# The first block's opening reordered by halves of the features

## The chip, the cores and the metric

The kernel runs on one core of one Trainium2 chip. The metric is device microseconds for one execution; lower is better. Engines are named as in the profile: PE is TensorE (PEld its weight loads), DVE is VectorE, ACT is ScalarE, POOL is GpSimd, SP is the engine that issues most transfers.

## The reference, cut to what matters

The kernel computes three transformer-like layers over 512 tokens of 1024 features. Only the opening of the first one matters here:

```python
mod = jax.nn.silu(c) @ w_ada + b_ada              # 1024 -> 3*1024
shift, scale, gate = jnp.split(mod, 3, axis=-1)
h = rms_norm(x, norm_g) * (1 + scale[:, None, :]) + shift[:, None, :]
proj = h @ w_in                                    # q, keys, values, gates, u, z
...
# u (512 columns) feeds the S5 mixer: tables from a_re, a_im, log_dt, b, c
lam_bar = jnp.exp(lam * dt)
b_bar = ((lam_bar - 1.0) / lam)[..., None] * lax.complex(b_re, b_im)
```

Products with `w_in` are made exact enough in float32 by splitting both operands into a rounded part (`hi`, type fp32r) and a remainder (`lo`), and adding three products: hi·hi, lo·hi, hi·lo.

## The kernel before

Each engine has its own list of instructions, written out by hand and run in order; semaphores join the lists. `x` comes in four token tiles of 128 rows. Features are counted in `KD` = 8 groups of 128, `k` = 0 to 7, so "the first half" is `k` = 0 to 3 (features 0 to 511).

**Modulation.** `w_ada` is cut into six pieces of 512 columns, 2048 KB each. Pieces 0 and 1 are the shift for the first and second half of the features, 2 and 3 the scale. `times_c` multiplies one piece by silu(c) on PE; ACT copies the resulting row out (`move_rows`, L676) and PE turns it into columns of `bank[4]` (`mod_columns`, with `ones`). DVE's `modulate` adds biases and writes `hT = hT * modA + modS`, one group `k` at a time (L1853, semaphore `h_raw`).

**Normalised x.** ACT squares the four token tiles with a running sum (L667, `ss`); POOL makes the inverse root (L539, L540); DVE scales (`normal`, L1803, `xn_ready`); PE transposes (L1133, `xT_done`); ACT moves the result to `hT` (L683, `xT_evac`).

**Splitting.** For each weight piece `n`, ACT writes `p_hi(n)` (L723) and DVE `p_lo(n)` (L1772). ACT rounds `hT` into `x_hi` (L731, `h_hi`), DVE writes the remainder into `hT_r` (L1865, `h_lower`).

**The linear unit.** The four tiles of `u` (PT_U + 0 to 3, 128 columns each, into banks 0 to 3) come first of all projections. Tile 0 is a plain float32 product of `hT` and the raw weights (eight matmuls, two records each in the trace); tiles 1 to 3 are `proj_T`, 24 matmuls each: eight of hi·hi, eight of lo·hi, eight of hi·lo. After them come two key/value tiles (`PT_KC`), `proj_tok` for `PT_KV` and `PT_KW`, the transposes of the S5 weights (`wt`, L1225, which wait for DVE's `wt_ready`), the products `kk` (which wait for `cl_ready` twice and ACT's `cl_moved`), `v`, and the queries, `PT_Q`, in four parts. From the last token tile of its part 1 on the queries carry `hidden_k`, and its first call has `pe.wait_ge(S["p_lo"], 15)`. Behind the queries PE waits for `state_ready`.

**Tables.** DVE's list holds, beside all this, the long computation of the S5 tables: angles (`turns`, three `less_turns` C1, C2, C3, `within`, `ang_ready`), powers (`pw`), and the products from `s2` on (first instruction at L1742, `small<-arena`), ending with `wt_ready`, `cl_ready` and, after the keys, `state_ready`. In the kernel before, the angles and powers stand ahead of `modulate(0)`. ACT's four sines stand ahead of the second `move_rows`.

Of the kernel before, what the change touches and what calls it, by code (L numbers as in the profile page):

```python
# [10 lines left out]
D = 1024  # L11
# [58 lines left out]
def build(nc, io):  # L70
# [8 lines left out]
    with ctx:  # L79
# [125 lines left out]
        ada_late = [cut(arena[:, n * SLOT:(n + 1) * SLOT], k=KD, n=512) for n in range(2)]  # L205
# [48 lines left out]
        def toe_of(g):  # L254
# [7 lines left out]
            "params_in", "x_in", "h_raw", "h_hi", "h_read", "p_hi", "p_lo", "p_used", "cl_moved", "k_stats", "k_rstd", "x_stats", "x_rstd", "xn_ready", "c_tanh", "c_silu", "ada_done", "mod_row",  # L262
            "tables_in", "za_ready", "gate_part", "gate_moved", "causal_in", "mod_cols", "h_lower", "half_evac", "gate_done", "gate_ready",
            "xT_done", "xT_evac", "proj_done", "proj_evac", "w_free", "dt_ready", "zr_ready", "em_ready", "sin_ready",
# [14 lines left out]
        ada_late_in = [sem(f"ada_late_in_{k}") for k in range(3)]  # L279
# [6 lines left out]
        chunks = [whole(ada[0]), whole(ada[1]),  # L286
# [9 lines left out]
        CH_U, CH_K, CH_KW, CH_Q, CH_W1, CH_ZS, CH_ZA, CH_GLU, CH_GATE, CH_WO = 2, 3, 4, 5, 6, 8, 9, 10, 11, 13  # L296

# [166 lines left out]
        def _(sp):  # L464
            for i in range(NT):
                sp.dma_start(x[:, i, :], io["x"][i * P:(i + 1) * P, :]).then_inc(S["x_in"], 16)
            for c, parts in enumerate(chunks):
                if c == CH_ZS:
                    continue
                if c >= SLOTS:  # L470
                    sp.wait_ge(S["w_free"], c - SLOTS + 1)
# [5 lines left out]
                if c == SLOTS - 1:  # L477
                    sp.dma_start(arena[:, 0:SLOT], ada[2]).then_inc(ada_late_in[0], 16)
                    for n in range(2):
                        sp.dma_start(arena[:, SLOT + 2048 * n:SLOT + 2048 * (n + 1)], ada[3][:, 2048 * n:2048 * (n + 1)]).then_inc(ada_late_in[1 + n], 16)  # L480
                elif c == CH_U:
# [47 lines left out]
        def _(pool):  # L529
# [17 lines left out]
            pool.wait_ge(S["x_stats"], 1)  # L547
# [101 lines left out]
        def _(act):  # L649
# [10 lines left out]
            act.activation(csl, col("c"), ACT.Tanh, scale=0.5).then_inc(S["c_tanh"], 1)  # L660
            act.activation(s1, col("log_dt"), ACT.Exp).then_inc(S["dt_ready"], 1)
# [3 lines left out]
            for i in range(NT):  # L665

                ins = act.activation(xn[:, i % 2, :], x[:, i, :], ACT.Square, accum_out=ss[:, i:i + 1])  # L667
                if i < NT - 1:
                    settle(ins)
# [4 lines left out]
            def move_rows(c):  # L674
                act.wait_ge(S["ada_done"], c + 1)
                act.activation(mod_rows[:, c * 512:(c + 1) * 512], bank[c][:, :], ACT.Copy).then_inc(S["mod_row"], 1)  # L676

            for i in range(NT):
                if i % 2 == 0:
                    move_rows(i // 2)  # L680
# [4 lines left out]
            act.wait_ge(S["ang_ready"], 1)  # L685
            act.activation(ang3[:, 0:160], ang[:, 0:160], ACT.Sin).then_inc(S["sin_ready"], 1)
            act.activation(ang2[:, 0:160], ang2[:, 0:160], ACT.Sin).then_inc(S["sin_ready"], 1)
            move_rows(2)
            act.activation(rot_s, ang[:, 160:1184], ACT.Sin).then_inc(S["sin_ready"], 1)
            act.activation(rot_c, ang2[:, 160:1184], ACT.Sin).then_inc(S["sin_ready"], 1)  # L690
# [5 lines left out]
            def part_hi(n):  # L696

                c = part1(n)[0]
                if n == 1:
                    act.wait_ge(u_ahead[1], 16)  # L700
                else:
                    act.wait_ge(arrive[c % SLOTS], landed(c))
                if 5 <= n < 8:
# [19 lines left out]
                act.activation(p_hi(n), p_raw(n), ACT.Copy).then_inc(S["p_hi"], 1)  # L723

            for k in range(KD):
                if k == 2:
                    move_rows(3)
                elif k == 4:
                    part_hi(1)
                act.wait_ge(S["h_raw"], k + 1)  # L730
                act.activation(x_hi[:, k, :], hT[:, k, :], ACT.Copy).then_inc(S["h_hi"], 1)  # L731
            for n in range(2, 5):
                part_hi(n)

            for f in range(4):
                src = proj(PT_U + f)[:, :].rearrange("p (n s) -> p s n", s=LC)
                act.activation(cut(uT[:, f * T:(f + 1) * T], s=LC, n=NCH), src, ACT.Copy).then_inc(S["proj_evac"], 1)
                if f:
                    part_hi(4 + f)
# [359 lines left out]
        def _(pe):  # L1099
# [13 lines left out]
            def mod_columns(c):  # L1113
                pe.wait_ge(S["mod_row"], c + 1)
                for k in range(4 * c, 4 * c + 4):
                    ins = mm(bank[4][:, k:k + 1], mod_rows[:, k * P:(k + 1) * P], ones[:, 0:1], True, True)
                return ins

            pe.wait_ge(S["params_in"], 32)
            pe.wait_ge(S["c_silu"], 1)  # L1120
            for c in range(4):
                if c < 2:
                    arrived(c)
                    times_c(bank[c], slot(c, KD, 512)).then_inc(S["ada_done"], 1)
                    pe.wait_ge(S["ada_done"], c + 1)
                    pe.sem_inc(S["w_free"], 1)
                    for i in range(2 * c, 2 * c + 2):
                        pe.wait_ge(S["xn_ready"], i + 1)
                        for b in range(2):
                            if i:  # L1130
                                pe.wait_ge(S["xT_evac"], 2 * i + b - 1)
                            for k in range(4):
                                ins = pe.transpose(bank[6 + b][:, k * P:(k + 1) * P], xn[:, i % 2, (4 * b + k) * P:(4 * b + k + 1) * P], ident)  # L1133
                            ins.then_inc(S["xT_done"], 1)
                elif c == 2:
                    pe.wait_ge(ada_late_in[0], 16)
                    times_c(bank[c], ada_late[0]).then_inc(S["ada_done"], 1)
                else:
                    for n in range(2):
                        pe.wait_ge(ada_late_in[1 + n], 16)  # L1140
                        ins = times_c(bank[c], ada_late[1], range(4 * n, 4 * n + 4))
                    ins.then_inc(S["ada_done"], 1)
                if c in (1, 2):
                    mod_columns(c - 1)
                if c == 2:
                    mod_columns(2).then_inc(S["mod_cols"], 1)
# [7 lines left out]
            def proj_T(p, n):  # L1154
# [4 lines left out]
                for k in range(KD):  # L1159
                    if k == 0:  # L1160
                        pe.wait_ge(S["p_hi"], n)
                    if p == 1:
                        pe.wait_ge(S["h_hi"], k + 1)
# [5 lines left out]
                for k in range(KD):  # L1169
                    if p == 1:  # L1170
                        pe.wait_ge(S["h_lower"], k + 1)
# [28 lines left out]
            pe.wait_ge(u_ahead[0], 16)  # L1200
            for k in range(KD):
                pe.wait_ge(S["h_raw"], k + 1)
                ins = mm(bank[0][:, :], p_raw(0)[:, k, :], hT[:, k, :], k == 0, k == KD - 1)
                if k < KD - 1:
                    ins.then_inc(S["h_read"], 1)
                if k == 0:
                    mod_columns(3).then_inc(S["mod_cols"], 1)
            ins.then_inc(S["proj_done"], 1)
# [1361 lines left out]
```

## Time and profile before

| | us |
|---|---|
| median of 3 runs | 911.82 (911.56 to 911.92) |
| profiled execution, its own time | 912.3 |
| its span, first to last instruction | 910.5 |
| mean granted TensorE clock | 0.997 |

The profiled execution took 1.8 us more than its span. "Start us, us" at the head of a timeline row is when a run of instructions began and how long it lasted; the square bracket is how long the engine had been idle before it and what ended that.

### The profile page before, as it was taken

What the parts mean: (1) busy time and instruction counts of PE and PEld (TensorE: products, weight loads), DVE (VectorE), ACT (ScalarE), POOL (GpSimd) and SP (SyncE); (2) the same over time, 40 slices, a digit from 0 to 9 for tenths busy, and PEclk for the clock granted to TensorE, in tenths of its full rate; (3) what the DMA queues carried; (4) which work ended last, traced back from release to release, by engine and by line L of the source; (5) the groups of instructions that cost most, each with busy time, mean ns of one, the idle gap of its engine ahead of it and who ended that gap; (6) DMA issues with size and microseconds to landing.
All of it is one profiled execution on the core that took longest, in us unless ns stands there. A gap on an engine that the chain in (4) does not pass through costs nothing.

```text
span 910.5 us, 14680 instructions
## 1 busy us (share of the span) xinstructions
PE 881.1 (97%) x5733; PEld 708.5 (78%) x5733; DVE 578.6 (64%) x1162; ACT 452.5 (50%) x956; POOL 97.9 (11%) x121
## 2 busy tenths in 40 slices
PE   3999999999999999999999999999999999999996
PEld 1579888784677778788888888888888888888885
DVE  5899797989887554666474455345476656445443
ACT  4724323476787333566525555334465544456531
POOL 1001111012300000000010222100000001123202
PEclk9999999999999999999999999999999999999998
DMA  9736646246200323323124332222422233333303
GB/s 384 329 98 139 182 150 187 105 144 226 93 2 2 116 87 113 111 72 116 48 93 138 117 116 89 68 93 93 130 77 72 88 127 105 99 91 112 94 0 93
DMA packets 34678, 104.69 MB, mean 115 GB/s; under 512 B 14961, under 2 KB 14961, under 8 KB 32178
## 3 DMA queue, kind: packets, MB, share of 16 engines
q1 hardware_dynamic: 28098, 85.77, 28.2%
q0 software_dynamic: 3856, 15.73, 5.5%
q10 hardware_dynamic: 2656, 2.26, 1.0%
q8 instruction: 46, 0.75, 0.3%
q14 instruction: 22, 0.18, 0.1%
HBM read 98.37 MB, written 4.19 MB: 113 GB/s over the span
## 4 chain that ended last, share of the span: by engine, by line
PE 92%; DVE 4%; ACT 2%; DMA 1%; issue 1%; SPq 0%; POOL 0%; POOLq 0%; ACTq 0%; DVEq 0%
PE bank L1104 85%; PE bank L1464 2%; PE bank L1444 2%; PE bank L1611 2%; DMA ring<-in_w_ada 1%; PE bank L1525 1%; DVE arena L1748 1%; PE bank L1515 0%; ACT arena L771 0%; DVE xn_t L2265 0%; DVE ring_lo L2289 0%; DVE w_lo L2234 0%; ACT soft L864 0%; DVE pw L1742 0%; DVE x_t L2325 0%
## 5 line engine op out<-in xcount | busy, mean ns | idle before, releaser
L2234 DVE TENSOR_TENSOR w_lo<-ring,w_hi 128x1024 fp32r<-128x1024 f32 x80 | 98.4, 1233 | 50.9 <-ACT w_hi L943 48.3
L1104 PE MATMUL bank<-hT_hi,w_hi 128*128 128x512 f32 x320 | 129.7, 405 | 0.0
L1104 PE MATMUL bank<-hT_lo,w_hi 128*128 128x512 f32 x320 | 125.1, 391 | 0.0
L1104 PE MATMUL bank<-hT_hi,w_lo 128*128 128x512 f32 x320 | 124.9, 390 | 0.0
L1104 PE MATMUL bank<-w_hi,hT_hi 128*128 128x512 f32 x256 | 102.0, 398 | 0.3 <-DVE hT_lo L2283 0.3
L1104 PE MATMUL bank<-w_lo,hT_hi 128*128 128x512 f32 x256 | 99.9, 390 | 0.0
L1104 PE MATMUL bank<-w_hi,hT_lo 128*128 128x512 f32 x256 | 99.8, 390 | 0.0
L943 ACT ACTIVATE w_hi<-ring 128x1024 fp32r<-128x1024 f32 x80 | 84.4, 1057 | 14.0 <-PE bank L1104 13.8
L1104 PEld LDWEIGHTS bank<-hT_hi,w_hi 128*128 128x128 f32 x320 | 60.1, 188 | 18.0 <-issue 4.7
L1104 PEld LDWEIGHTS bank<-hT_lo,w_hi 128*128 128x128 f32 x320 | 60.1, 188 | 13.3
L1104 PEld LDWEIGHTS bank<-hT_hi,w_lo 128*128 128x128 f32 x320 | 60.2, 188 | 11.1
L2179 DVE CUSTOM_DVE_ANT_0 ring<-bank,bias_ring 128x512 f32<-128x512 f32 x64 | 40.4, 687 | 35.5 <-PE bank L1104 25.7
L1104 PEld LDWEIGHTS bank<-w_hi,hT_hi 128*128 128x128 f32 x256 | 48.1, 188 | 12.1 <-issue 2.7
L948 ACT ACTIVATE bank<-x_t 128x512 f32<-128x512 f32 x24 | 14.4, 602 | 86.4 <-DVE x_t L2455 53.1
L890 ACT ACTIVATE ring<-ring,small 128x512 f32<-128x512 f32 x64 | 45.5, 713 | 21.6 <-DVE small L2179 21.6
L1104 PEld LDWEIGHTS bank<-w_lo,hT_hi 128*128 128x128 f32 x256 | 48.0, 188 | 10.4
L1104 PEld LDWEIGHTS bank<-w_hi,hT_lo 128*128 128x128 f32 x256 | 48.1, 188 | 9.3
L1104 PE MATMUL bank<-arena 128*64 128x64 f32 (+5 forms) x688 | 52.2, 286 | 0.1
L1004 ACT ACTIVATE ring<-ring,small 128x256 f32<-128x256 f32 x64 | 31.8, 498 | 31.6 <-DVE small L2340 31.6
L1104 PEld LDWEIGHTS bank<-arena 128*64 128x64 f32 (+1 forms) x688 | 36.3, 146 | 10.3 <-issue 7.2
L2340 DVE CUSTOM_DVE_ANT_0 ring<-bank,bias_ring 128x256 f32<-128x256 f32 x64 | 23.3, 421 | 31.8 <-PE bank L1104 31.8
L608 POOL TENSOR_TENSOR ring<-ring,small 128x512 f32<-128x512 f32 x32 | 33.0, 1046 | 94.6 <-DVE small L2348 94.4
(340 smaller groups left out, 1838.5 us busy)
## 6 DMA issues: line engine op xcount, KB each, us to landing
ring<-in_w_units SPq DMA_DIRECT2D x80, 512.0 KB, 3.7
ring<-in_w_ada SPq DMA_DIRECT2D x4, 2048.0 KB, 10.3
bias_ring<-in_na_bias POOLq DMA_DIRECT2D x6, 1024.0 KB, 5.3
ring<-in_w_out SPq DMA_DIRECT2D x2, 2048.0 KB, 8.7
bias_ring<-in_t_bias POOLq DMA_DIRECT2D x8, 448.0 KB, 3.6
x_t<-in_x SPq DMA_DIRECT2D x4, 512.0 KB, 5.7
arena<-in_w_ada SPq DMA_DIRECT2D x1, 2048.0 KB, 20.0
arena<-in_w_ada SPq DMA_DIRECT2D x2, 1024.0 KB, 22.9
```

Source lines behind the costliest of these rows:

```text
L608: pool.tensor_tensor(p, p, r, MUL).then_inc(S["na_scaled"], 1)
L890: act.activation(p, p, ACT.Exp, scale=-1.0, bias=negm[:, k % 8:k % 8 + 1], accum_out=ssum[:, k % 8:k % 8 + 1])\
L943: act.activation(w_hi[:, u % 4], raw_w[:, u % 4], ACT.Copy).then_inc(S["w_hi_ready"], 1)
L948: settle(act.activation(place[:, 0:n], x[:, i, c0:c0 + n], ACT.Square, scale=scale, accum_out=ssq[:, part * NT + i:part * NT + i + 1]))
L1004: act.activation(p, p, ACT.Exp, scale=-1.0, bias=negm[:, k % 16:k % 16 + 1], accum_out=ssum[:, k % 16:k % 16 + 1])\
L1104: return pe.matmul(out, lhsT, rhs, start=first, stop=last)
L1444: ins = pe.transpose(bank[0][:, b * P:(b + 1) * P], src[:, b * P:(b + 1) * P], ident)
L1464: ins = pe.transpose(bank[k % 2][:, b * P:(b + 1) * P], prob1_of(k)[:, b * P:(b + 1) * P], ident)
L1611: ins = pe.transpose(bank[m % 2][:, at_], prob2[:, m % 8, at_], ident)
L2179: dve.tensor_tensor_reduce(prob_of(k)[:, 0:width], bank[D_BANKS[k % 4]][:, 0:width], bias, -scale, 3.0e38, ADD, MIN, negm[:, k % 8:k % 8 + ...
L2234: dve.tensor_tensor(w_lo[:, u % 4], raw_w[:, u % 4], w_hi[:, u % 4].bitcast(fp32), SUB).then_inc(S["w_split"], 1)
L2340: dve.tensor_tensor_reduce(prob2[:, m % 8, e * KW:(e + 1) * KW], na_scores(m, e), bias_ring[:, n % 2, at_:at_ + KW], -1.0, 3.0e38, ADD, MI ...
```

## The change

- **Transfers.** Piece 0 goes to `arena`, piece 2 (scale of the first half) to `cl`, then the four `w_u` tiles, then piece 1, then, once PE has used piece 0 (`ada_done` 1), piece 3 into the place of piece 0. `w_k` waits for `w_free` 2, which PE now gives after the first half of tile 2.
- **Statistics.** ACT squares token tiles 0 and 1, DVE tiles 2 and 3 with `tensor_tensor_reduce`; POOL waits for both.
- **PE's list.** Transposes of token tiles 0 and 1, piece 0, transposes 2 and 3, its columns, piece 2, its columns; then the first half of tiles 0 and 1; piece 1; first half of tile 2; its columns; first half of tile 3; piece 3; its columns; then the second half of all four tiles. Tile 0 is now split like the others.
- **DVE's list.** `modulate(0)`, the remainders of `hT` 0 to 3, `p_lo` 1 to 3, C3, `modulate(1)`, the remainders 4 to 7; only then `within`, the rest of the angles, the powers, and the table products as before.
- **ACT's list.** The four sines come after the rounding of the second half.

The core of the diff:

```diff
-            for c, parts in enumerate(chunks):
+            sp.dma_start(arena[:, 0:SLOT], ada[0]).then_inc(ada_late_in[0], 16)
+            sp.dma_start(cl[:, 0:SLOT], ada[2]).then_inc(ada_late_in[1], 16)
+            for c in (CH_U, 1, *range(CH_K, len(chunks))):
...
+                if c == 1:
+                    sp.wait_ge(S["ada_done"], 1)
                     for n in range(2):
+                        sp.dma_start(arena[:, 2048 * n:2048 * (n + 1)], ada[3][:, 2048 * n:2048 * (n + 1)]).then_inc(ada_late_in[2 + n], 16)
...
+            move_hT(0)
+            move_hT(1)
+            move_rows(0)
+            move_hT(2)
+            move_hT(3)
+            part_hi(0)
+            move_rows(1)
+            part_hi(1)
+            round_x(0)
+            part_hi(2)
+            part_hi(3)
+            move_rows(2)
+            move_rows(3)
+            round_x(1)
+            act.wait_ge(S["ang_ready"], 1)
...
+            def u_half(f, half):
+
+                ks = range(4 * half, 4 * half + 4)
+                pe.wait_ge(S["p_hi" if f else "u0_hi"], max(f, 1))
+                for k in ks:
+                    if f == 0:
+                        pe.wait_ge(S["h_hi"], k + 1)
+                    mm(bank[f][:, :], p_hi(f)[:, k, :], x_hi[:, k, :], k == 0, False)
+                pe.wait_ge(S["p_lo" if f else "u0_lo"], max(f, 1))
+                for k in ks:
+                    mm(bank[f][:, :], p_lo(f)[:, k, :], x_hi[:, k, :], False, False)
+                for k in ks:
+                    if f == 0:
+                        pe.wait_ge(S["h_lower"], k + 1)
+                    ins = mm(bank[f][:, :], p_hi(f)[:, k, :], hT_r[:, k, :], False, k == KD - 1)
+                if half:
+                    ins.then_inc(S["proj_done"], 1)
...
+            mod_columns(1).then_inc(S["mod_cols"], 1)
+            u_half(0, 0)
+            u_half(1, 0)
+            arrived(1)
+            pe.wait_ge(S["xT_evac"], 2 * NT)
+            times_c(bank[ROW_PLACE[2]], slot(1, KD, 512)).then_inc(S["ada_done"], 1)
+            u_half(2, 0)
+            pe.wait_ge(S["ada_done"], 3)
+            pe.sem_inc(S["w_free"], 2)
+            mod_columns(2)
+            u_half(3, 0)
+            for n in range(2):
+                pe.wait_ge(ada_late_in[2 + n], 16)
+                ins = times_c(bank[ROW_PLACE[3]], ada_late[0], range(4 * n, 4 * n + 4))
+            ins.then_inc(S["ada_done"], 1)
+            mod_columns(3).then_inc(S["mod_cols"], 1)
+            for f in range(4):
+                u_half(f, 1)
...
-            pe.wait_ge(u_ahead[0], 16)
-            for k in range(KD):
-                pe.wait_ge(S["h_raw"], k + 1)
-                ins = mm(bank[0][:, :], p_raw(0)[:, k, :], hT[:, k, :], k == 0, k == KD - 1)
...
+            dve.wait_ge(S["x_in"], 16 * NT)
+            for i in range(2, NT):
+                ins = dve.tensor_tensor_reduce(hT_t[:, (i - 2) * D:(i - 1) * D], x[:, i, :], x[:, i, :], 1.0, 0.0, MUL, ADD, ss[:, i:i + 1])
+            ins.then_inc(S["x_stats"], 1)
...
+            modulate(0)
+            lower_x(0)
+            part_lo(1)
+            part_lo(2)
+            part_lo(3)
             less_turns(ang, ang2, C3)
+            modulate(1)
+            lower_x(1)
             within(ang)
             stt(ang2, ang, -1.0, ang, MUL, MAX)
             dve.tensor_scalar(ang2, ang2, -1.0, math.pi / 2, MUL, ADD).then_inc(S["ang_ready"], 1)
```

## Rows read from the trace of the kernel before

**Rows 1.** The page: busy time by engine, and the chain that ended last.
```profile
PE 881.1 (97%) x5733; PEld 708.5 (78%) x5733; DVE 578.6 (64%) x1162; ACT 452.5 (50%) x956; POOL 97.9 (11%) x121
...
PE 92%; DVE 4%; ACT 2%; DMA 1%; issue 1%; SPq 0%; POOL 0%; POOLq 0%; ACTq 0%; DVEq 0%
```

**Rows 2.** The chain, 0 to 150 us: start, length, what.
```profile
2.72 11.29 DMA ring<-in_w_ada
...
33.25 23.91 PE bank L1104 x94
...
97.02 33.30 PE bank L1104 x416
...
130.76 6.17 PE bank L1104 x204
```

**Rows 3.** PE's timeline, 0 to 110 us.
```profile
14.14 3.64 PE L1104 MATMUL bank<-ring,csl_pad 128*32 128x512 f32 x16 [14.14 <-DMA ring<-in_w_ada]
...
20.57 1.92 PE L1104 MATMUL bank<-ring,csl_pad 128*32 128x512 f32 x16
...
24.27 1.06 PE L1133 MATMUL bank<-cons,xn_t 128*128 128x128 f32 x8 [0.34 <-ACT hT_t L683]
...
33.25 1.05 PE L1104 MATMUL bank<-ones,soft 128*128 128x1 f32 x8 [0.48 <-ACT soft L676]
34.16 6.25 PE L1104 MATMUL bank<-hT_t,ring 128*128 128x512 f32 x14
...
43.97 2.04 PE L1104 MATMUL bank<-hT_r,a_hi 128*128 128x512 f32 x8
45.85 2.03 PE L1104 MATMUL bank<-x_hi,a_hi 128*128 128x512 f32 x8
```

**Rows 4.** DVE's timeline, 0 to 110 us.
```profile
12.37 1.59 DVE L1745 TENSOR_SCALAR arena<-arena 128x1184 f32<-128x1184 f32 x2
15.41 1.42 DVE L1803 TENSOR_SCALAR xn_t<-x_t,small 128x1024 f32<-128x1024 f32 x2 [1.45 <-POOL small L540]
...
23.52 0.78 DVE L1745 TENSOR_SCALAR arena<-arena 128x1184 f32<-128x1184 f32 x1
...
30.38 0.17 DVE L1742 TENSOR_TENSOR small<-bank,cols 128x8 f32<-128x8 f32 x1
...
30.98 1.92 DVE L1853 TENSOR_SCALAR hT_t<-hT_t,small 128x512 f32<-128x512 f32 x4
...
37.70 4.90 DVE L1865 TENSOR_TENSOR hT_r<-hT_t,x_hi 128x512 fp32r<-128x512 f32 x8
...
44.79 0.17 DVE L1742 TENSOR_TENSOR small<-arena 128x16 f32<-128x16 f32 x1
...
87.33 2.55 DVE L1933 TENSOR_TENSOR arena<-cq,arena 64x2304 f32<-64x2304 f32 x1
...
102.96 0.69 DVE L2007 COPY soft<-small 128x1024 f32<-128x1024 f32 x1 [0.78 <-PE bank L1104]
```

**Rows 5.** ACT's timeline, 0 to 110 us.
```profile
22.56 0.60 ACT L676 ACTIVATE soft<-bank 128x512 f32<-128x512 f32 x1 [1.24 <-PE bank L1104]
...
35.31 2.20 ACT L731 ACTIVATE x_hi<-hT_t 128x512 fp32r<-128x512 f32 x4
```

**Rows 6.** Transfers issued from 0 to 60 us: count, KB each, median us to landing.
```profile
arena<-in_w_ada SPq DMA_DIRECT2D x2, 1024.0 KB, 22.9
...
ring<-in_w_kw SPq DMA_DIRECT2D x1, 1120.0 KB, 6.6
```

**Rows 7.** DVE in one stretch: stretch, length, busy.
```profile
44.79:95.99 51.20, 49.85 (x57) 1.00 0.47 115
```

**Rows 8.** DVE's timeline, 95 to 175 us.
```profile
110.78 1.22 DVE L1772 TENSOR_TENSOR ring_lo<-ring,a_hi 128x1024 fp32r<-128x1024 f32 x1
...
124.31 4.91 DVE L1742 TENSOR_TENSOR arena<-arena 64x1008 f32<-64x1008 f32 x4
```

**Rows 9.** PE's timeline, 98 to 132 us.
```profile
114.04 1.15 PE L1104 MATMUL bank<-xn_t,ring 128*64 128x66 f32 x32
```

More of the change, by code:

```diff
@@ L204, in build @@
         mod_rows = soft[:, 0:2 * D]
-        ada_late = [cut(arena[:, n * SLOT:(n + 1) * SLOT], k=KD, n=512) for n in range(2)]
+        ada_late = [cut(v[:, 0:SLOT], k=KD, n=512) for v in (arena, cl)]
+        ADA = [0, 2, 1, 3]
         gate_part = cl[:, 4096:4608]
@@ L664, in _ @@
             act.wait_ge(S["x_in"], 16 * NT)
[L665 to L669, printed above, removed]
+            for i in range(2):
+                ins = act.activation(xn[:, i, :], x[:, i, :], ACT.Square, accum_out=ss[:, i:i + 1])
             ins.then_inc(S["x_stats"], 1)
@@ L672, in _, with move_rows, move_hT @@
             act.activation(th, zr, ACT.Tanh, scale=0.5).then_inc(S["em_ready"], 1)
[L674 to L680, printed above, removed]
+            def move_rows(n):
+                act.wait_ge(S["ada_done"], n + 1)
+                act.activation(mod_rows[:, ADA[n] * 512:(ADA[n] + 1) * 512], bank[ROW_PLACE[n]][:, :], ACT.Copy).then_inc(S["mod_row"], 1)
+            def move_hT(i):
                 for b in range(2):
@@ L722, in part_hi, with round_x @@
                     act.wait_ge(S["proj_done"], PT_ZA + n - 21)
-                act.activation(p_hi(n), p_raw(n), ACT.Copy).then_inc(S["p_hi"], 1)
-            for k in range(KD):
[L726 to L733, printed above, removed]
+                act.activation(p_hi(n), p_raw(n), ACT.Copy).then_inc(S["p_hi" if n else "u0_hi"], 1)
+            def round_x(half):
+                for k in range(4 * half, 4 * half + 4):
+                    act.wait_ge(S["h_raw"], k + 1)
+                    act.activation(x_hi[:, k, :], hT[:, k, :], ACT.Copy).then_inc(S["h_hi"], 1)
+            move_hT(0)
[13 more added lines that the diff above has]
+            act.wait_ge(S["ang_ready"], 1)
+            act.activation(ang3[:, 0:160], ang[:, 0:160], ACT.Sin).then_inc(S["sin_ready"], 1)
+            act.activation(ang2[:, 0:160], ang2[:, 0:160], ACT.Sin).then_inc(S["sin_ready"], 1)
+            act.activation(rot_s, ang[:, 160:1184], ACT.Sin).then_inc(S["sin_ready"], 1)
+            act.activation(rot_c, ang2[:, 160:1184], ACT.Sin).then_inc(S["sin_ready"], 1)
             for f in range(4):
@@ L1119, in _ @@
             pe.wait_ge(S["params_in"], 32)
+            turn_x(0)
+            turn_x(1)
             pe.wait_ge(S["c_silu"], 1)
[L1121 to L1146, printed above, removed]
@@ L1816, in _, with modulate, lower_x @@
             normal(1)
+            turns(ang2, ang)
+            normal(2)
             less_turns(ang, ang2, C1)
-            normal(2)
+            normal(3)
             less_turns(ang, ang2, C2)
-            normal(3)
+            part_lo(0)
+            b_ada = col("b_ada")
+            dve.wait_ge(S["xT_evac"], 2 * NT)
+            def modulate(half):
+                dve.wait_ge(S["mod_cols"], half + 1)
+                ks = slice(4 * half, 4 * half + 4)
+                tt(modS[:, ks], bank[4][:, ks], b_ada[:, ks], ADD)
+                stt(modA[:, ks], bank[4][:, KD + 4 * half:KD + 4 * half + 4], 1.0, b_ada[:, KD + 4 * half:KD + 4 * half + 4], ADD, ADD)
+                tt(modA[:, ks], modA[:, ks], col("norm_g")[:, ks], MUL)
+                for k in range(4 * half, 4 * half + 4):
+                    dve.tensor_scalar(hT[:, k, :], hT[:, k, :], modA[:, k:k + 1], modS[:, k:k + 1], MUL, ADD).then_inc(S["h_raw"], 1)
+            def lower_x(half):
+                for k in range(4 * half, 4 * half + 4):
+                    dve.wait_ge(S["h_hi"], k + 1)
+                    dve.tensor_tensor(hT_r[:, k, :], hT[:, k, :], x_hi[:, k, :].bitcast(fp32), SUB).then_inc(S["h_lower"], 1)
+            modulate(0)
[3 more added lines that the diff above has]
+            part_lo(3)
             less_turns(ang, ang2, C3)
+            modulate(1)
+            lower_x(1)
             within(ang)
```

102 lines of the change are left out of this document (36 added, 66 removed).

## The prediction

> **What bounds the kernel now.** I read the page first. PE is busy for 97% of the span and makes up 92% of the chain that ended last [rows 1]. So the question is what PE waits for in the opening, and whether anything else could become the bound. The chain in order of time comes next. A transfer holds everything until about 14 us, and from 33.25 us on the chain is almost only PE: 23.91 us to the end of the linear unit, then on through the keys and queries to 130.32, a pause of 0.44 us, and on [rows 2]. Whatever delays PE between 33 and 130 us delays the end by as much; the chain names no slack to take it up.
>
> PE's timeline then says how much a better opening could win. PE starts at 14.14 and ends the linear unit at 57.16 [rows 2, 3]; its idle times in brackets there are 0.17 to 0.48 us each, about 2 us in all. So the opening is not a row of waits into which work can be put. It is PE work nearly end to end.
>
> The timeline of DVE matters as much. The tables (23.52 to 30.38) were done before the modulation, in time in which DVE had nothing more pressing. From 44.79 on DVE works without a break to 95.99, 49.85 of 51.20 us busy [rows 4, 7]. A list that dense gives nothing back if it starts later. Its slack to PE is small in two places: `p_lo(15)` is ready at 110.78 + 1.22 = 112.00 and PE wants it at 114.04 [rows 8, 9]; `state_ready` comes at 124.31 + 4.91 = 129.22 and PE passes it at 130.76 [rows 2, 8].
>
> **The change, part by part.**
>
> *Prices.* Eight matmuls of 512 columns take 45.85 − 43.97 = 1.88 us, so half a tile (12) takes 2.8 us [rows 3]. Piece products take 1.9 us when warm, eight transposes 0.9 us, four columns 1.0 us [rows 3]. ACT rounds a group in 2.20/4 = 0.55, DVE modulates one in 0.48 and writes a remainder in 0.61 [rows 4, 5]. Moving a row costs PE about 0.7 (0.60 and the hand-overs) [rows 5].
>
> *Start.* DVE gets two squares with a sum. The trace has none of 1024 columns; a plain DVE operation on 1024 takes 1.22 [rows 8], and nothing cheaper is likely. Free would be the lower bound, twice that the upper; I take 1.27 each. DVE was free at 13.96 (15.41 less its 1.45 idle). With 2.5 added and `turns` (1.59) moved behind `normal`, it starts `normal(0)` at about 15.0 and the first transposes start at 15.8 [rows 4]. That is 1.7 later than PE's start before, since the piece that PE had worked on at 14.14 now comes second.
>
> *PE to the first half of h.* At 1.2 GHz the first sixteen records took 3.64, later ones 1.92 [rows 3], so I price the first 16 transposes double: to 19.5. Piece 0 to 21.4; sixteen transposes with one wait for ACT to 23.6; columns to 24.6; piece 2 to 26.4; row move and columns to 28.2. `modulate(0)` needs 0.6 for its three small operations and 0.56 for the first group, ACT 0.6: PE restarts at 30.1. The idle 1.9 is new.
>
> *Tile halves and the second modulation.* The first four matmuls go at ACT's 0.55, then eight at 0.23: 33.8. First half of tile 1 to 36.6, piece 1 to 38.4, half of tile 2 to 41.2, columns to 42.1, half of tile 3 to 44.9, piece 3 to 46.8, row move to 47.5, columns to 48.5. Before, the last columns ended at 34.30 [rows 3]. **The second half's modulation becomes 14.2 us later**, because two pieces now stand behind four half tiles. No transfer decides this: piece 3 waits for piece 0's use at 21.4, but all `w_ada` and `w_u` bytes had landed by 35 us before, piece 3 by about 28 [rows 6], and the total is the same.
>
> *End of the unit.* `modulate(1)` and ACT again: PE restarts at 50.4 (idle 1.9), 52.3, 54.1 for tile 0, three more halves of 2.8: 62.5 to 62.9. Before: 57.16. The new split of tile 0 is in this: 24 matmuls, 5.6, for a plain float32 product of some 6.85 (14 of its 16 records took 6.25) [rows 3], a gain of 1.2. **PE alone: about 5.5 later.** `w_k` is asked for at 41.2; 1120 KB on an idle queue took 6.6 [rows 6], 2048 KB at that rate 12.1, so it lands by 53.3 and ACT wants it only after its sines, near 59.5: hidden.
>
> *DVE.* Here is the larger loss. `modulate(1)` stands ahead of the rest of the tables in DVE's list, and DVE cannot pass it. After C3 (37.9) DVE idles to 48.6, some 10.7 us, with 6.9 us of tables waiting behind. Then 0.6 + 1.8 + 2.4 gives 53.4 at the end of the remainders, and 6.86 of angles and powers (23.52 to 30.38 [rows 4]) 60.3. ACT's short sines are inside that. The point that was at 44.79 is at 60.3: **+15.5**. The dense stretch carries this whole to 95.99, POOL's root too. The 0.78 that DVE waited for PE at 102.96 is absorbed [rows 4]: +14.7 from there.
>
> *Where PE meets it.* `cl_ready` 2 ended at 89.88 [rows 4]; at 105.4 it is past PE's 97.02 [rows 2] + 5.5, so `kk` starts at 105.4 and PE is at +8.4. (ACT's copies that wait for `wt_ready` hold up the emptying of banks for PT_KW on the way there.) `p_lo(15)` comes at 112.0 + 14.7 = 126.7, PE is there at 114.04 + 8.4 = 122.4: a stall of 4.3, +12.7. `state_ready` comes at 129.22 + 14.7 = 143.9; PE goes on at 144.0 instead of 130.76: **+13.3**. From there DVE waits for PE again before 140 in the old count, and both move on by the same amount.
>
> *Sum.* 910.5 + 13.3 = 923.8 of span; the profiled execution 912.3 + 13.3 = 925.6; against the median of the runs, 911.8 + 13.3 = 925.1. I forecast **925.1**.
>
> **Rivals.**
>
> *The lag of DVE is absorbed.* If slack I don't see takes up DVE's 15.5 us, only PE's own 5.5 count: 917.3. For it speaks that only two places are tight; against it that both lie in rows 8 and 9 with 2.0 and 1.5 us of slack against 14.7 − 5.5 = 9.2. Chance 0.10; 0.05 more for stopping at `kk`'s +8.4, 920.2.
>
> *Faster: the waits are all covered.* PE's work itself becomes less: tile 0 gives 1.2, and the double price at the start falls on transposes of 1.8 instead of a piece of 1.9. If the second modulation were ready when PE asks (`h_hi` 5 by 48.5 instead of 50.3, likewise at 28.2), PE's end of the unit would be at 62.7 less two pauses of 1.9, two row moves of 0.7 and 1.8 for the matmuls that go at ACT's pace, 55.7 instead of 57.16: a gain of 1.5, 910.3. It decides only if the last columns end by 34.3 + 2 (DVE's slack), that is, if four half tiles of 11.2 us do not stand before them. They do. Chance 0.03.
>
> *TensorE's clock falls in the new pauses.* The clock column reads 1.00 throughout, yet the first sixteen records after PE's long idle ran at the 1.2 GHz pace, 3.64 against 1.92 [rows 3]. The new pauses are 1.9, 1.9 and 4.3. If a pause costs as much as that first stretch, it is 1.7 each; the first delays `mod_cols` and so all of DVE, the third eats the 0.6 between stall and `state_ready`: 1.7 + 1.1 = 2.8, 927.9. Chance 0.15.
>
> The Trainium skill, "TensorE: Matmul & The Clock Gate", Part 1, says that half rate is PE's default state and that an idle PE is gated back to it; it speaks against any order that opens pauses. By that rule the last rival would be the rule and not the exception; by the rows of the opening before, whose pauses after 14 us are all shorter than 1 us, it can be neither shown nor denied.
>
> **How the numbers follow.** My forecast 0.64, DVE absorbed 0.10, stop at `kk` 0.05, clock 0.15, faster 0.03, no change within 0.2% (1.8 us, about what a measurement can tell) 0.03. The unknown prices move the forecast little: the squares by −2.5 to +2.5 if they were free or double, the start's clock by ±1.5. The range runs from 919.0, which keeps the `kk` case, to 929.5, the clock case with 1.6 on top. Faster 0.03, same 0.03, slower 0.94.
>
> **What would show it.** Right: the last `bank<-ones,soft` group ends near 48.5; DVE shows one idle of about 10 us before the second modulation, released by PE; the first PT_KC matmul starts near 63; PE waits for DVE before `kk`, before the first `bank<-xn_t,ring` group, and before `state_ready`. Wrong: no idle on DVE in 38 to 48 us (then the lists run otherwise than I read them), PE at `kk` less than 7 us late, or 128x512 records of twice the length after a pause.

## The result, and the profile after

The changed kernel takes **929.88 us** (median of 6 runs, 929.59 to 930.39) against 911.87 for the kernel before on the same chip (6 runs, 911.39 to 912.99). The ratio is 1.0196, with an interval of 1.0183 to 1.0210: slower by 18.0 us, where 13.3 were forecast and the range ended at 929.5. The direction and most of the size were right; the time lies 0.4 us above the range.

The page of the kernel after, beside [rows 1]: busy time by engine, the granted clock in 40 slices, the shares of the chain.

```profile
PE 887.1 (96%) x5741; PEld 715.2 (77%) x5741; DVE 582.2 (63%) x1168; ACT 450.8 (49%) x953; POOL 97.3 (10%) x121
...
PEclk9989989999999999999999999999999999999999
...
PE 85%; DVE 11%; issue 1%; ACT 1%; DMA 1%; POOL 0%; SPq 0%; POOLq 0%; DVEq 0%; ACTq 0%
```

The span is 927.8 us, 17.3 longer than before; the medians are 18.0 apart, because the profiled execution before took a little more than its median (912.3) and the one after a little less (929.59). PE's busy time grew by 6.0 though the linear unit holds less matmul work, and DVE's share of the chain rose from 4% to 11%. Two things are to be explained: who makes PE wait, and why PE's own work takes longer.

PE's timeline of the kernel after, 0 to 110 us (start, length, instruction, and in brackets the idle time before it and who ended it), beside [rows 3]:

```profile
15.97 3.81 PE L1133 MATMUL bank<-cons,xn_t 128*128 128x128 f32 x16 [15.97 <-DVE xn_t L1824]
19.71 2.51 PE L1112 MATMUL bank<-arena,csl_pad 128*32 128x512 f32 x16
...
28.02 1.05 PE L1112 MATMUL bank<-ones,soft 128*128 128x1 f32 x8 [0.72 <-ACT soft L678]
31.12 2.27 PE L1112 MATMUL bank<-x_hi,a_hi 128*128 128x512 f32 x4 [2.06 <-ACT x_hi L722]
33.19 1.74 PE L1112 MATMUL bank<-x_hi,ring_lo 128*128 128x512 f32 x4
34.77 1.09 PE L1112 MATMUL bank<-hT_r,a_hi 128*128 128x512 f32 x4
...
49.70 1.05 PE L1112 MATMUL bank<-ones,soft 128*128 128x1 f32 x8 [0.72 <-ACT soft L678]
52.81 2.27 PE L1112 MATMUL bank<-x_hi,a_hi 128*128 128x512 f32 x4 [2.06 <-ACT x_hi L722]
54.87 1.91 PE L1112 MATMUL bank<-x_hi,ring_lo 128*128 128x512 f32 x4
56.58 1.91 PE L1112 MATMUL bank<-hT_r,a_hi 128*128 128x512 f32 x4
58.29 1.20 PE L1112 MATMUL bank<-x_hi,a_hi 128*128 128x512 f32 x4
...
67.19 2.10 PE L1112 MATMUL bank<-x_hi,a_hi 128*128 128x512 f32 x8 [0.30 <-PE bank L1112]
```

The two `bank<-ones,soft` groups shown are the last columns of each modulation. The second ends at 49.70 + 1.05 = 50.75; before, the last columns ended at 34.30 [rows 3]. Behind each, PE waits 2.06 us. No idle time of PE in this timeline was ended by a transfer. And behind each wait the next groups are slow: four matmuls take 1.91 at 54.87 and again at 56.58, where four of the same kind take 1.09 at 34.77. The windows name the cause (stretch, its length, busy time and count for PE, PEld, DVE, ACT and POOL, granted TensorE clock, DMA share, GB/s):

```profile
32.00:36.00 4.00, 4.00 (x13) 3.04 (x13) 4.00 (x6) 2.43 (x4) 0.00 (x0) 0.67 0.97 398
36.00:40.00 4.00, 4.00 (x28) 2.23 (x26) 2.80 (x3) 0.00 (x0) 0.00 (x0) 1.00 0.00 1
...
52.00:56.00 4.00, 3.19 (x7) 2.29 (x8) 4.00 (x8) 3.48 (x5) 0.00 (x0) 0.50 0.00 2
56.00:60.00 4.00, 4.00 (x13) 3.13 (x13) 3.69 (x10) 1.26 (x3) 0.00 (x0) 0.69 0.00 0
60.00:64.00 4.00, 4.00 (x19) 3.23 (x18) 3.41 (x18) 4.00 (x6) 0.00 (x0) 1.00 0.01 4
...
128.00:132.00 4.00, 2.86 (x34) 2.67 (x35) 3.93 (x4) 0.00 (x0) 0.00 (x0) 0.50 0.00 0
```

After each pause the granted clock is at 0.50, which is the 1.2 GHz level, for some microseconds, and then back at 1.00, the 2.4 GHz level. The first window above is a mean over both levels: taken alone, 32 to 34 us read 0.50 and 35 to 36 read 1.00.

DVE's timeline of the kernel after, 0 to 155 us, beside [rows 4, 8]:

```profile
9.46 1.22 DVE L1829 CUSTOM_DVE_ANT_0 hT_t<-x_t 128x1024 f32<-128x1024 f32 x1 [0.20 <-DMA x_t<-in_x]
...
37.41 1.39 DVE L1769 SCALAR_TENSOR_TENSOR arena<-arena 128x1184 f32<-128x1184 f32 x1
50.86 0.16 DVE L1763 TENSOR_TENSOR small<-bank,cols 128x4 f32<-128x4 f32 x1 [12.06 <-PE bank L1112]
...
62.52 0.18 DVE L1763 TENSOR_TENSOR small<-arena 128x16 f32<-128x16 f32 x1
...
105.05 2.55 DVE L1959 TENSOR_TENSOR arena<-cq,arena 64x2304 f32<-64x2304 f32 x1
...
127.77 1.22 DVE L1793 TENSOR_TENSOR ring_lo<-ring,a_hi 128x1024 fp32r<-128x1024 f32 x1
...
141.30 4.92 DVE L1763 TENSOR_TENSOR arena<-arena 64x1008 f32<-64x1008 f32 x4
```

This is the idle time that the prediction asked for: 12.06 us of DVE waiting for PE's last columns, with the tables queued behind. The dense stretch starts at 62.52 instead of 44.79, +17.7, and carries it along: `p_lo(15)` ends at 128.99 instead of 112.00, `state_ready` comes at 146.22 instead of 129.22, both +17.0.

PE's timeline around there, and the chain in order of time, beside [rows 9, 2]:

```profile
129.14 2.03 PE L1112 MATMUL bank<-xn_t,ring 128*64 128x66 f32 x32 [4.38 <-DVE ring_lo L1793]
...
147.88 0.34 PE L1112 MATMUL bank<-arena,soft 128*64 128x64 f32 x4 [0.45 <-PE bank L1112]
```

```profile
129.14 18.30 PE bank L1112 x176
147.88 5.90 PE bank L1112 x195
```

PE waits 4.38 for `p_lo(15)`, and then does until 147.44 what took from 114.04 to 130.32 before: 18.30 us instead of 16.28. It goes on at 147.88 instead of 130.76, +17.12, and from there to the end the difference stays.

### The profile page after: what moved, and what is told of

Its sections match the earlier page's. It is cut to its first block, busy times and chain, and to the rows that moved or that the text cites. A ratio compares the mean times of both kernels' runs of the same rounds, so it can differ in the third digit from the quotient of the medians.

```text
span 927.8 us, 14696 instructions
## 1 busy us (share of the span) xinstructions
PE 887.1 (96%) x5741; PEld 715.2 (77%) x5741; DVE 582.2 (63%) x1168; ACT 450.8 (49%) x953; POOL 97.3 (10%) x121
## 4 chain that ended last, share of the span: by engine, by line
PE 85%; DVE 11%; issue 1%; ACT 1%; DMA 1%; POOL 0%; SPq 0%; POOLq 0%; DVEq 0%; ACTq 0%
PE bank L1112 78%; DVE arena L1763 3%; PE bank L1485 2%; PE bank L1465 2%; PE bank L1632 2%; DVE ring_lo L1793 1%; DMA x_t<-in_x 1%; PE bank L1546 1%; DVE cq L1763 1%; PE bank L1133 1%; POOL small L545 0%; PE bank L1536 0%; DVE soft L1763 0%; DVE small L1763 0%; DVE arena L1959 0%
## 5 line engine op out<-in xcount | busy, mean ns | idle before, releaser
L1112 PEld LDWEIGHTS bank<-w_hi,hT_hi 128*128 128x128 f32 x256 | 48.1, 188 | 12.0 <-issue 2.7
L956 ACT ACTIVATE bank<-x_t 128x512 f32<-128x512 f32 x24 | 14.4, 602 | 86.4 <-DVE x_t L2481 53.1
L898 ACT ACTIVATE ring<-ring,small 128x512 f32<-128x512 f32 x64 | 45.5, 713 | 21.6 <-DVE small L2205 21.6
L1112 PEld LDWEIGHTS bank<-w_hi,hT_lo 128*128 128x128 f32 x256 | 48.1, 188 | 9.4
```

Source lines behind the costliest of these rows:

```text
L898: act.activation(p, p, ACT.Exp, scale=-1.0, bias=negm[:, k % 8:k % 8 + 1], accum_out=ssum[:, k % 8:k % 8 + 1])\
L1112: return pe.matmul(out, lhsT, rhs, start=first, stop=last)
```

## The experiments

Ten kernels, in three groups; the ratio is to the kernel before, measured again beside each group on the same chip. Its medians were 912.38 us for the first four kernels of the table, 912.46 for the next four and 912.07 for the last two. All times are medians in us.

| kernel | time | ratio and interval |
|---|---|---|
| tables_first | 921.60 | 1.0102 [1.0087, 1.0117] |
| pieces_early | 922.83 | 1.0113 [1.0098, 1.0128] |
| both_orders | 921.48 | 1.0102 [1.0085, 1.0119] |
| before_tables_late | 917.50 | 1.0057 [1.0042, 1.0072] |
| two_pauses_filled | 928.41 | 1.0179 [1.0165, 1.0193] |
| three_pauses_filled | 926.87 | 1.0158 [1.0144, 1.0172] |
| orders_and_place | 915.68 | 1.0038 [1.0024, 1.0052] |
| best_order | 912.19 | 1.0000 [0.9992, 1.0009] |
| turns_covered | 911.20 | 0.9991 [0.9982, 1.0000] |
| turns_covered_small_first | 913.06 | 1.0017 [1.0008, 1.0026] |

### The order of DVE's list: tables_first

The changed kernel with the rest of the tables ahead of the second modulation, and ACT's four sines between its last two row moves, so that both run while DVE otherwise idles.

```diff
             less_turns(ang, ang2, C3)
-            modulate(1)
-            lower_x(1)
             within(ang)
...
             ts(pw_nim, pw_im, -1.0, None, MUL, ALU.bypass)
+            modulate(1)
+            lower_x(1)
             tt(s2, sn[:, 144:160], sn[:, 144:160], MUL)
```

> The changed kernel, but DVE's remaining angles and powers stand ahead of the second modulation, and ACT's four sines between the third and the fourth row move. PE's list is untouched. Theory A (DVE's list order is the larger loss: it idles 12 us with 6.9 us of tables behind it): DVE's small table products start near 55.7 instead of 62.5, the waits of PE for DVE at kk, at the first hidden product and at state_ready go, PE keeps its +9.7 at the end of the linear unit: 921.6, between 920.5 and 923. Theory B (only PE's order counts, DVE's lag is absorbed): no change, 929.9.

Measured 921.60. That is 8.3 less than the changed kernel (8.6 by the ratios, 1.0102 against 1.0196), though PE's opening is nearly the same: its first PT_KC matmul starts at 66.42 instead of 67.19. DVE's timeline of this kernel, 35 to 72 us:

```profile
50.21 0.16 DVE L1763 TENSOR_TENSOR small<-bank,cols 128x4 f32<-128x4 f32 x1 [5.07 <-PE bank L1112]
...
59.47 1.23 DVE L1793 TENSOR_TENSOR ring_lo<-ring,a_hi 128x1024 fp32r<-128x1024 f32 x1 [1.24 <-ACT a_hi L717]
```

The idle time before the modulation fell from 12.06 to 5.07 us, by the 7.0 of tables that now run in it. So 8 of the 18 us of the change were the place of one step in DVE's list. There is no pause before the hidden product any more; from there on PE waits 0.84 us at `state_ready` alone. The second line is a wait that the changed kernel did not have: `p_lo(4)` wants `p_hi(4)`, and ACT may write that only when tile 0's sums are finished.

### The order of PE's list: pieces_early

The changed kernel with the pieces of the second modulation and their columns ahead of the half tiles 2 and 3 on PE; DVE's list as changed.

```diff
-            u_half(2, 0)
-            pe.wait_ge(S["ada_done"], 3)
-            pe.sem_inc(S["w_free"], 2)
-            mod_columns(2)
-            u_half(3, 0)
             for n in range(2):
...
+            mod_columns(2)
+            pe.wait_ge(S["ada_done"], 3)
+            pe.sem_inc(S["w_free"], 2)
             mod_columns(3).then_inc(S["mod_cols"], 1)
+            u_half(2, 0)
+            u_half(3, 0)
```

> The changed kernel, but PE multiplies the two pieces of the second half and makes their columns before the first halves of tiles 2 and 3 instead of around them. DVE's and ACT's lists are untouched. Theory A (the second modulation is late because half tiles stand before its pieces, and the lateness of DVE passes to the end): last columns end near 44.2 instead of 50.8, the linear unit ends near 61, the whole chain of DVE moves by 6.5: 923.4, between 922 and 925. Theory B (the end is set by PE's order alone): the unit ends near 61 instead of 66.8, so 924. Theory C (the transfers of the pieces set it): the last piece has not landed, nothing moves, 929.9.

Measured 922.83. DVE's list now restarts at 44.13, 6.7 earlier, and the time falls by 7.1 (by the ratios, 1.0113 against 1.0196, 7.6). PE's timeline of this kernel, 105 to 155 us:

```profile
122.43 2.03 PE L1112 MATMUL bank<-xn_t,ring 128*64 128x66 f32 x32 [4.39 <-DVE ring_lo L1793]
141.64 0.34 PE L1112 MATMUL bank<-arena,soft 128*64 128x64 f32 x4 [0.45 <-PE bank L1112]
```

The long pause before the hidden product is still there, and the queries behind it take 18.77 us. `state_ready` came at 134.59 + 4.92 = 139.51; with queries of 16.28 us [rows 2, 9] PE would have been done before it, at 138.71. It was done at 141.20, and these 1.7 us behind `state_ready` are the clock's.

### Both together: both_orders

The two edits above in one kernel.

> Both edits together: pieces early on PE, tables first on DVE. Theory A: the unit ends about 4 us later than in the kernel before, DVE's small products start near 50.5, 5.7 later, of which 0.8 and 1.5 are slack; the end is set by PE's 4: 916, between 914.5 and 918. Theory B (DVE without effect): as with the pieces early alone, 923 to 924.

Measured 921.48, a miss by 5.5 us: no better than tables_first alone. ACT's timeline (38 to 60 us) and DVE's (35 to 72 us) of this kernel:

```profile
41.23 1.28 ACT L737 ACT_TABLE_LOAD   x1
...
42.99 1.04 ACT L739 ACTIVATE arena<-arena 128x1024 f32<-128x1024 f32 x1
43.94 1.04 ACT L740 ACTIVATE arena<-arena 128x1024 f32<-128x1024 f32 x1
44.88 0.57 ACT L678 ACTIVATE soft<-bank 128x512 f32<-128x512 f32 x1
```

```profile
59.59 1.23 DVE L1793 TENSOR_TENSOR ring_lo<-ring,a_hi 128x1024 fp32r<-128x1024 f32 x1 [4.09 <-ACT a_hi L717]
```

Two things ate the gain. The sines stand ahead of the fourth row move in ACT's list, and with PE's pieces early they are no longer beside half tiles: PE waits 2.27 us for that row, and the granted clock is 0.62 from 44 to 48 us and 0.53 from 48 to 52. And the wait for `p_hi(4)` grew to 4.09: `p_hi(4)` is written to the place of `p_hi(0)`, which is free only when tile 0 is whole, here at 57.9. Since the change makes every tile end late, this place is a third thing that can hold DVE's list back. It does not bind in the changed kernel itself, where DVE comes to it at 65.75.

### The place: orders_and_place

Both orders, the sines behind both row moves, and `p_hi(4)` and `p_hi(5)` in a place of their own, so that ACT can write `p_hi(4)` right after its sines and rounding.

```diff
+            c_hi = cut(sbm("c_hi", 2 * UNIT)[:, :], u=2, n=UNIT)
...
-                return CH_K, KD, 512, slice(0, KD), slice((n - 4) * P, (n - 3) * P), b_hi[:, n - 4]
+                return CH_K, KD, 512, slice(0, KD), slice((n - 4) * P, (n - 3) * P), c_hi[:, n - 4]
...
-                if 4 <= n < 8:
+                if 6 <= n < 8:
                     act.wait_ge(S["proj_done"], PT_U + n - 3)
```

> As both orders together, but ACT's sines stand behind both row moves of the second half (there they held up the last columns and opened a pause of 2.3 us), and p_hi 4 and 5 have places of their own, so that the split of w_k doesn't wait for tile 0 and 1 to be finished (in the run with both orders DVE waited 4.1 us for p_hi(4)). Theory A with these two further waits: last columns end near 44, the unit ends 3.6 us later than in the kernel before, DVE's small products start near 50.5 and don't wait: 915.8, between 914.5 and 917. Rival (something else holds the halves' order at +9): 921.5.

Measured 915.68, as expected, 5.8 less than both_orders: the two causes named there are right together (their shares were not measured one by one). DVE has no wait in 35 to 72 us any more.

### The second reason by itself, without the change: before_tables_late

The kernel before with one edit: angles, powers and sines moved behind the modulation, the remainders of `h` and `p_lo(1)` to `p_lo(3)`, on DVE and ACT. PE's list and all products are those of before.

> The kernel before, but with the angles, powers and sines moved behind the modulation, the remainders and p_lo 1 to 3 (6.9 us on DVE), as the changed kernel has them; PE's list, transfers and statistics are untouched. Theory A (DVE's list from 44.8 us on has only about 1.5 us of slack at state_ready): DVE's chain moves by 6.9, less the 0.8 it waited for PE; p_lo(15) is 4 us late for the first hidden product; the end moves by 4.6 if TensorE keeps its clock in that pause and by 6.1 if it falls to 1.2 GHz: 916.5 or 918.0. Theory B (the lag is absorbed): 911.9.

Measured 917.50, +5.1 us (912.38 before, ratio 1.0057), between the two values expected. The small products start at 50.62 instead of 44.79, 5.8 later; it is not 6.9, because DVE takes up the first columns 1.0 earlier (29.39 instead of 30.38), about half of it since the tables no longer hold it there and half since PE's first records ended sooner in this execution. PE's linear unit ends 1.0 earlier too (PT_KC starts at 56.45 instead of 57.45), and the kernel is slower all the same. PE's timeline, its windows and the chain of this kernel:

```profile
117.25 2.03 PE L1104 MATMUL bank<-xn_t,ring 128*64 128x66 f32 x32 [4.14 <-DVE ring_lo L1772]
```

```profile
109.00:113.00 4.00, 4.00 (x18) 3.00 (x16) 3.86 (x6) 0.00 (x0) 0.00 (x0) 1.00 0.68 102
...
117.00:121.00 4.00, 3.75 (x36) 3.36 (x37) 3.93 (x4) 0.00 (x0) 0.00 (x0) 0.50 0.00 0
```

```profile
117.25 18.78 PE bank L1104 x176
```

A later list on DVE alone, with nothing of the split in it, makes the kernel slower by nearly its whole lag, and it makes the same pause and the same slow queries: 18.78 us where 16.28 were needed at the full clock. PE had been at work without a break at clock 1.00 up to the pause.

### The clock: two_pauses_filled, three_pauses_filled

The changed kernel with matmuls whose result nobody reads put into the pauses: two plain float32 products of 512 columns ahead of the first and ahead of the second restart of tile 0 (they do not wait for `h`), and in the second kernel four more before the first hidden product, once `p_lo(14)` is there.

```diff
+            def keep_busy(b, n):
+
+                for k in range(n):
+                    mm(bank[b][:, :], ident, cons[:, 0:512], True, True)
...
             mod_columns(3).then_inc(S["mod_cols"], 1)
+            keep_busy(6, 2)
...
+                        pe.wait_ge(S["p_lo"], 14)
+                        keep_busy(4, 4)
                         pe.wait_ge(S["p_lo"], 15)
```

> The changed kernel with four added matmuls whose result nobody reads (plain float32, 128x512, about 0.85 us each): two into bank 6 in the pause before the first half of tile 0, two in the pause before its second half. Everything else is as in the changed kernel. Theory A (TensorE's clock fell in these pauses, and the first fall delays the second modulation and so all of DVE): the 4.6 us of the first half tile become 3.7, the last columns end 0.9 earlier, 929.0; the second fall is off DVE's chain and gives nothing more. Rival (the clock's fall costs nothing at the end, or the added matmuls are late and cost their own time): 929.9 or more.

> As the run with two pauses filled, and four more unread matmuls into bank 4 in the 4.4 us pause before the first hidden product of the keys. Theory A: the queries behind it take 16.3 us as in the kernel before instead of 18.3, so PE is ready before state_ready and the end is then set by DVE alone: 2.4 to 2.5 less than the changed kernel, 927.4. Rival (that stretch was not on the path that sets the end): 929.0 as with two.

Measured 928.41 and 926.87, ratios 1.0179 and 1.0158 against 1.0196. More work on PE makes the kernel faster, by 3.5 us with all three pauses filled. How this splits is less sure. By the ratios the first two pauses give 1.5 us and the third 1.9, but the interval with two filled (1.0165 to 1.0193) overlaps that of the changed kernel (1.0183 to 1.0210), and the spans of the profiled executions (927.8, 927.1, 925.0) say 0.7 and 2.1. The span's mean clock rises from 0.990 to 0.995 and 0.998, and in both kernels it reads 1.00 in every window from 28 to 40 and from 48 to 60 us. In the first of the two kernels PT_KC starts 3.0 us earlier (64.23), but DVE's list only 1.0 (49.83 instead of 50.86), and the time does not fall by 3.0 either; it follows DVE. PE's timeline of three_pauses_filled, 105 to 155 us:

```profile
128.50 1.16 PE L1112 MATMUL bank<-xn_t,ring 128*64 128x66 f32 x32 [0.28 <-DVE ring_lo L1803]
145.87 0.34 PE L1112 MATMUL bank<-arena,soft 128*64 128x64 f32 x4 [1.12 <-DVEq L2068]
```

The 32 narrow matmuls take 1.16 instead of 2.03, and now it is `state_ready` (140.75 + 4.92 = 145.67) that PE waits for. This is the kernel that the sum of the prediction was made for, one without falls of the clock, and it is at +14.4 where the sum said +13.3.

### An order that costs nothing: best_order, turns_covered, turns_covered_small_first

best_order starts from orders_and_place. The squares go back to ACT. PE starts with piece 0 at 14.17 and does piece 1 before any tile. Piece 3 comes behind the half tiles 0 and 1, half tile 2 covers its row move, and half tile 3 stands behind the last columns and covers the second modulation. On DVE the angles are done between the normalizations, and the small products too come before the second modulation.

```diff
             times_c(bank[ROW_PLACE[0]], ada_late[0]).then_inc(S["ada_done"], 1)
+            turn_x(0)
+            turn_x(1)
...
+            u_half(0, 0)
+            u_half(1, 0)
...
             u_half(2, 0)
+            mod_columns(3).then_inc(S["mod_cols"], 1)
             u_half(3, 0)
```

> The halves rearranged by what the runs showed: PE starts with piece 0 at 14 us as in the kernel before, then the transposes; all four squares on ACT; piece 1 lands before the last w_u tiles and is multiplied in the first pause; piece 3 before the first half of tiles 2 and 3; DVE does all angles, powers and the small products ahead of the second modulation; own places for p_hi 4 and 5. If the losses are only those found (late second modulation, DVE's list, pauses with the clock's fall, p_hi(4)), PE ends the linear unit near 56.3 instead of 57.2 and DVE is on its old schedule: 911.0, between 910 and 912.5. If the halves' order costs by itself, 914 or more.

Measured 912.19, ratio 1.0000 [0.9992, 1.0009]: the whole loss is gone, and nothing is won, where 911.0 had been expected. PT_KC starts at 57.27 (57.45 before) and PE passes `state_ready` at 130.59 (130.76 before). The granted clock reads 1.00 from 20 to 52 us, where PE's longest pause is 0.72 us.

turns_covered moves piece 0's columns and piece 2's product between the transposes and ACT's `part_hi(0)` forward. On DVE two table steps go behind `p_lo(3)`, and the small products go behind `modulate(1)`.

```diff
-            turn_x(2)
-            turn_x(3)
             mod_columns(0)
+            turn_x(2)
             pe.wait_ge(ada_late_in[1], 16)
             times_c(bank[ROW_PLACE[1]], ada_late[1]).then_inc(S["ada_done"], 1)
+            turn_x(3)
             mod_columns(1).then_inc(S["mod_cols"], 1)
```

> The best order so far, with the waits of the transposes filled: columns of piece 0 and the product of piece 2 stand between the transposes of the token tiles, ACT splits w_u 0 earlier, DVE leaves the last two angle operations for after p_lo 3 and the small products for after the second modulation. In the run before, PE waited 0.34 three times and 0.72 once there. If these are on the path, PE restarts on tile 0 about 1.2 earlier, and if DVE's list (small products now 1.2 us later, PE 1.2 us earlier, against slack of 0.8 + 1.5) just keeps up: 911.2, between 910.5 and 912. Rival (DVE's list becomes the bound at state_ready again): 911.9 or more.

Measured 911.20, as expected, ratio 0.9991 [0.9982, 1.0000], which can hardly be told from no change. PE's timeline of this kernel, 40 to 75 and 105 to 155 us, and DVE's, 110 to 160 us:

```profile
55.90 2.10 PE L1122 MATMUL bank<-x_hi,c_hi 128*128 128x512 f32 x8 [0.30 <-PE bank L1122]
...
130.20 0.34 PE L1122 MATMUL bank<-arena,soft 128*64 128x64 f32 x4 [1.02 <-DVEq L2064]
```

```profile
125.08 4.92 DVE L1773 TENSOR_TENSOR arena<-arena 64x1008 f32<-64x1008 f32 x4
```

PE gains 1.5 us by the end of the unit, the gain that the prediction's rival "faster" named. But `state_ready` comes at 130.00, 0.8 later than before, and PE waits 1.02 for it. It goes on at 130.20 instead of 130.76: two thirds of the gain are given back to DVE's list.

turns_covered_small_first has the tables' small products ahead of `modulate(1)` again, as best_order had, to start DVE's dense stretch earlier.

> The same, but the small products stay ahead of the second modulation on DVE. Then DVE's chain is on the old schedule, but the second modulation starts about 1.5 us later than its columns are there and PE waits for it before the second half of tile 0: between 911.2 and 912.3; better than the other order only if DVE was the bound there.

Measured 913.06, ratio 1.0017 [1.0008, 1.0026], a miss on the high side by 0.8. PE's timeline (14 to 60 us) and the windows of this kernel, and ahead of them the same product in turns_covered:

```profile
26.34 1.92 PE L1122 MATMUL bank<-ring,csl_pad 128*32 128x512 f32 x16
```

```profile
26.52 2.93 PE L1122 MATMUL bank<-ring,csl_pad 128*32 128x512 f32 x16 [1.16 <-DMA ring<-in_w_ada]
```

```profile
24.00:28.00 4.00, 2.84 (x26) 1.78 (x28) 3.34 (x10) 3.54 (x7) 0.96 (x4) 0.91 0.99 418
28.00:32.00 4.00, 4.00 (x17) 2.16 (x10) 4.00 (x7) 3.35 (x5) 0.00 (x0) 0.66 1.01 420
```

PE waited 1.16 us for piece 1, and the piece's product took 2.93 instead of 1.92; the clock in the next window is 0.66. The piece was not late: issue and time to landing give 4.93 + 21.4 = 26.3 in turns_covered and 4.89 + 21.6 = 26.5 here. PE was early. Its slow first records ended sooner in this execution (piece 0 took 3.28 instead of 3.64, the transposes behind it ran at full pace), so it was through with the columns at 25.36 instead of 26.29. In turns_covered it came to the piece just as this landed, which is luck. PE restarts on tile 0 at 29.39 instead of 28.37, and PT_KC starts at 57.39, 1.5 later than in turns_covered and where it starts in the kernel before. So this takes away the gain, but it does not explain a time above the kernel before: the profiled execution passes `state_ready` at 130.71 (130.76 before) and took 912.66, while the eleven runs reach up to 914.95. The list of DVE that was to be tried has its effect behind this (`state_ready` at 129.81 instead of 130.00) and was not read apart from it. What makes the longer executions long is open.

## Why the prediction fell short

- **What bounds the kernel** [rows 1 to 3]: right. Every delay of PE in 33 to 130 us came out at the end; +17.1 at `state_ready`'s product, +17.3 of span.
- **Squares and start**: right. The square with its sum took 1.22 (1.27 assumed), plus 0.08 to read the sum; PE started at 15.97 (15.8).
- **PE to the first half of h**: 1.0 too small. The columns ended at 29.07 (28.2). 0.6 of it is piece 0, which was priced at full pace and took 2.51, not 1.92. Tile 0 restarted at 31.12 (30.1), after an idle of 2.06 (1.9). The prediction puts the slow first records down to the 1.2 GHz level. Their length fits that, but no granted clock shows it: it reads 1.00 there in both kernels (14 to 19 us before, 16 to 22 us in this one).
- **Half tiles**: the split itself was priced rightly (half tile 1 took 2.77 for 2.8), but the first half tile took 4.74 instead of 3.7, because the clock was at half rate behind the pause. The last columns ended at 50.75, not 48.5: about half from the start and half from this.
- **End of the unit**: 66.89, not 62.5 to 62.9. 2.4 of it came down from above, the rest is tile 0 at the 1.2 GHz level again after the second pause. PE alone was at +9.7 and not +5.5. It had little effect on the time, since PE still came to `kk` 0.50 before DVE was there.
- **DVE**: right in kind and, from its start on, in every length. Idle 12.06 (10.7); from the columns to the small products 11.7 (11.7); +17.7 where +15.5 was said, the difference being the columns' 2.25. tables_first and before_tables_late show the cause by itself. The 0.78 absorbed was right (+17.0 after +17.7). `w_k` landed at 48.1, 7.5 after its issue (53.3 said, scaled up by bytes), and held nobody.
- **Where PE meets it**: the places were right. `kk` started at 107.7, +10.7 (8.4 said, with the same 2.3 missing); the stall before the hidden product was 4.38 (4.3 said).
- **`state_ready` → +13.3**: this step failed. DVE's part came at +15.6, the 2.3 again. But PE was not there: the queries behind the stall took 18.30 and not 16.28, and ended 1.2 us after `state_ready`. PE passed at +17.1.

The terms of the miss: 1.0 of the start (0.6 of it the slow pace of piece 0), 1.0 to 1.2 for the clock behind the first pause, 1.6 behind the third; 3.8 in all, which is 13.3 against 17.1. The mechanism was right, DVE's late list and the places where PE meets it. The step that failed was to put the fall of the clock behind the new pauses at nothing in the sum; the runs showed 2.6 to 2.8 us for it in the trace, and 3.5 by the kernels whose pauses were filled. It stood among the rivals with 0.15 and a price of 2.8, "1.7 each; the first delays `mod_cols` and so all of DVE, the third eats the 0.6 between stall and `state_ready`", which is what happened, place by place. So its price was nearly right, and its chance, in hindsight, too low. With it the forecast would have been 927.9, and with the 1.0 of the start 928.9; most of the rest to 929.88 is the 0.7 between medians and profiled executions. The Trainium skill, "TensorE: Matmul & The Clock Gate", Part 1, calls half rate the default state to which an idle PE returns. All three long pauses here agree with it, with 0.50 behind each; the prediction cited this and gave it a small chance because the kernel before had no pause in which it could show.

Of the other rivals, "DVE's lag is absorbed" fell (not one of the two tight places gave more than the counted slack), and "faster" fell for the changed kernel for the reason given, four half tiles in front of the last columns; turns_covered shows that its 1.5 us of PE exist. **The gain found for the split is about 1.5 us at PT_KC, and DVE's list, which is dense up to `state_ready`, takes back 1.0 of it.** What remains open is what makes some executions of turns_covered_small_first longer, and how the two causes in both_orders share the 5.8.

## What to carry to other kernels

When PE's work is reordered so that one engine's input comes later, look at what stands behind the waiting step in that engine's list: here 7 us of tables that needed nothing from PE stood behind it and cost 8.3 of the 18 us. A pause that a plan opens on PE, above all in the opening, is to be priced as the pause plus the slow matmuls behind it (here 1 to 2.5 us each), in the sum and not as a rival, even if the kernel before shows a full clock everywhere. Buffers that are freed by a finished tile come free late when all tiles are started by halves; list them before the order is changed.

## What the runs showed of the hardware

- Pauses of 2.06, 2.27, 4.14 and 4.38 us of PE were each followed by windows at a granted clock of 0.50 to 0.67; 16.28 us of queries became 18.30 to 18.78.
- The length of the pause alone does not say whether the clock falls. Behind 1.16 us between the columns and the product of piece 1 it fell (0.66, turns_covered_small_first); behind 1.66 us at 88.92 in two_pauses_filled it read 1.00, and so it did behind 0.72 in the opening of best_order.
- The clock fell after 4.14 us of pause even behind a stretch in which PE had been busy without a break at 1.00.
- Unread matmuls in three pauses took 3.5 us off the time.
- The first sixteen matmul records take 3.64 us (before) and 3.81 (changed), about twice what the same work takes later, while the granted clock reads 1.00: that column does not show every slow stretch.
- On DVE a product of 1024 float32 columns with its sum takes 1.22 us and 0.08 to read the sum, no more than a plain operation of that size.
